# Projection groups of four parts over four PSUM banks in a one-core decoder step

## What is computed

```python
def run_trunk(x, mem_k, mem_v, states, P):
        y, mix_state = mixer_block(rmsnorm(x, P['norm_mix'][l]), ...)      # GLA, mLSTM, S5 branches
        x = x + y                                                          # y = merged @ w_out
        x = x + cross_attn(rmsnorm(x, P['norm_cross'][l]), mem_k[l], mem_v[l], P['w_cq'][l], P['w_co'][l])
        f, conv_state = conv_ffn(rmsnorm(x, P['norm_ffn'][l]), s_conv, P['w_ffn_up'][l],
                                 P['ffn_conv_w'][l], P['ffn_conv_b'][l], P['w_ffn_down'][l])
        x = x + f
    y = rmsnorm(x, P['norm_final'])

# in mixer_block:
    merged = (sigmoid(za) * (y_a @ w_branch_a) + sigmoid(zb) * (y_b @ w_branch_b)
              + sigmoid(zc) * (y_c @ w_branch_c))                          # the "branch gates"
```

## Time and profile before

| | us |
|---|---|
| median of 3 runs | 2227.8 |
| lowest and highest run | 2226.13, 2229.34 |
| span of the profiled execution | 2224.6 |
| TensorE matmul busy in it | 2183.2 (98%) |
| VectorE busy | 1157.5 (52%) |
| ScalarE busy | 605.2 (27%) |
| GpSimd busy | 281.4 (13%) |

### The profile page before, as it was taken

One profiled execution on the slowest core, in us unless ns is written; L12 is line 12 of the kernel. 1 busy time (PEld: TensorE's weight loads), 2 busy tenths in 40 slices (PEclk: granted clock), 3 DMA queues, 4 the chain that ended last, 5 costly groups with the idle time before them and its releaser, 6 DMA issues.

```text
span 2224.6 us, 34095 instructions
## 1 busy us (share of the span) xinstructions
PE 2183.2 (98%) x14582; PEld 2137.4 (96%) x14582; DVE 1157.5 (52%) x1336; ACT 605.2 (27%) x765; POOL 281.4 (13%) x436
## 2 busy tenths in 40 slices
PE   7999999999999999999999999999999999999997
PEld 6999999999999999999999988999999999999997
DVE  6514755344455354245643234456566665656657
ACT  6313344233322322333322144221111111111113
POOL 6689910000000000000000000000000000000001
PEclk9999999999999999999999999999999999999998
DMA  7322114212422223245312161111111111111112
GB/s 277 114 76 69 63 59 170 78 68 84 148 98 77 86 74 111 76 162 181 124 48 77 46 257 75 39 58 48 48 48 48 48 41 48 46 48 48 48 48 81
DMA packets 51872, 191.39 MB, mean 86 GB/s; under 512 B 5984, under 2 KB 11424, under 8 KB 48528
## 3 DMA queue, kind: packets, MB, share of 16 engines
q1 hardware_dynamic: 39232, 125.47, 16.5%
q0 software_dynamic: 10496, 46.66, 5.6%
q10 hardware_dynamic: 2016, 17.35, 2.0%
HBM read 152.53 MB, written 35.93 MB: 85 GB/s over the span
## 4 chain that ended last, share of the span: by engine, by line
PE 93%; DVE 4%; ACT 1%; DMA 1%; issue 1%; POOL 0%; DVEq 0%; ACTq 0%; POOLq 0%
PE ps L272 27%; PE ps L273 26%; PE ps L275 26%; PE ps L1939 1%; PE ps L2291 1%; PE ps L2267 1%; DVE WL L266 1%; DMA WRAW<-in_wslabs 1%; PE ps L2301 1%; ACT WH L261 1%; DVE XR L2781 0%; PE ps L1123 0%; PE ps L1124 0%; PE ps L1118 0%; DVE T L1009 0%
## 5 line engine op out<-in xcount | busy, mean ns | idle before, releaser
L272 PE MATMUL ps<-XH,WH 128*128 128x344 f32 x1752 | 563.5, 324 | 5.1 <-ACT STAGE L331 2.8
L273 PE MATMUL ps<-XL,WH 128*128 128x344 f32 x1560 | 495.1, 320 | 0.0
L272 PE MATMUL ps<-XN,WH 128*128 128x344 f32 x1224 | 391.0, 321 | 0.2 <-DVE WL L266 0.2
L273 PE MATMUL ps<-XN,WH 128*128 128x344 f32 x1224 | 389.3, 321 | 0.0
L275 PE MATMUL ps<-XH,WL 128*128 128x344 f32 x1752 | 371.4, 320 | 0.0
L266 DVE TENSOR_TENSOR WL<-WRAW,WH 128x1024 fp32r<-128x1024 f32 x177 | 220.8, 1248 | 277.0 <-ACT WH L261 276.3
L272 PEld LDWEIGHTS ps<-XH,WH 128*128 128x128 f32 x1752 | 330.2, 188 | 13.8 <-issue 9.3
L261 ACT ACTIVATE WH<-WRAW 128x1024 fp32r<-128x1024 f32 x177 | 186.6, 1054 | 517.6 <-PE ps L275 499.3
L273 PEld LDWEIGHTS ps<-XL,WH 128*128 128x128 f32 x1560 | 294.3, 189 | 0.1
L275 PEld LDWEIGHTS ps<-XH,WL 128*128 128x128 f32 x1752 | 293.6, 188 | 0.0
L275 PE MATMUL ps<-XN,WL 128*128 128x344 f32 x1224 | 259.0, 319 | 0.0
(11 more groups left out here) (542 smaller groups left out, 3163.8 us busy)
## 6 DMA issues: line engine op xcount, KB each, us to landing
WRAW<-in_wslabs SPq DMA_DIRECT2D x177, 512.0 KB, 3.5
scratch_spill<-STAGE SPq DMA_DIRECT2D x40, 516.0 KB, 2.7
ZS<-scratch_spill POOLq DMA_DIRECT2D x24, 516.0 KB, 5.4
XIN<-in_xT SPq DMA_DIRECT2D x8, 516.0 KB, 4.5
XR<-in_xT ACTq DMA_DIRECT2D x2, 2064.0 KB, 8.8
out_y<-XR SPq DMA_DIRECT2D x12, 344.0 KB, 2.5
CACHES<-in_ck ACTq DMA_DIRECT2D x4, 1024.0 KB, 14.2
CACHES<-in_cv ACTq DMA_DIRECT2D x4, 1024.0 KB, 16.0
```

The lines of the kernel that those rows point to most:

```text
L272: pe.matmul(out[t], WH[:, slot, w, :], xh(k, t), start=(k == 0), stop=False)
L273: pe.matmul(out[t], WH[:, slot, w, :], xl(k, t), start=False, stop=False)
```

## The change

From the branch gates on, most groups are made of `WIDE` = 4 parts of 258 columns in four banks, so slot 0 has banks 0 to 3 and slot 1 banks 4 to 7, all eight. A step of such a group has twelve matmuls and twelve weight loads. Helpers take the number of parts. Still of three parts are: all groups before the gates, the last group of `w_out` and of `w_co`, the first two and the last of the query projection, the first two of `w_co`, the first two of the FFN, and the last chunk's down product. Since slot 1 now holds banks 6 and 7, TensorE waits for `norm_rb` before the first four-part group of the query projection and of the FFN. VectorE's loop over the query groups is written out.

```diff
-TG, NTG = 344, 3
+TG, NTG, WIDE = 344, 3, 4
-        def acc(slot):
-            return ps[:, 3 * slot:3 * slot + 3, 0:TG]
-        def t3(ap):
-            return ap.rearrange("p (a b) -> p a b", b=TG)
+        def acc(slot, parts=NTG):
+            return ps[:, parts * slot:parts * (slot + 1), 0:N // parts]
+        def t3(ap, parts=NTG):
+            return ap.rearrange("p (a b) -> p a b", b=N // parts)
         def split_step(pe, out, slot, xh, xl, w, k, nk):
-            for t in range(len(out)):
-                pe.matmul(out[t], WH[:, slot, w, :], xh(k, t), start=(k == 0), stop=False)
-                pe.matmul(out[t], WH[:, slot, w, :], xl(k, t), start=False, stop=False)
-            for t in range(len(out)):
-                last = pe.matmul(out[t], WL[:, slot, w, :], xh(k, t), start=False, stop=(k == nk - 1))
+            parts = len(out)
+            for t in range(parts):
+                pe.matmul(out[t], WH[:, slot, w, :], xh(k, t, parts), start=(k == 0), stop=False)
+                pe.matmul(out[t], WH[:, slot, w, :], xl(k, t, parts), start=False, stop=False)
+            for t in range(parts):
+                last = pe.matmul(out[t], WL[:, slot, w, :], xh(k, t, parts), start=False, stop=(k == nk - 1))
+        def banks(slot, parts=NTG):
+            return [ps[:, parts * slot + t, 0:N // parts] for t in range(parts)]
+        def cols(t, parts=NTG):
+            return slice(t * (N // parts), (t + 1) * (N // parts))
...
         def pe_out(pe):
-            pe_start(pe, SL_OUT, G_OUT, 2, xl_cols)
-            pe_project(pe, SL_OUT + 2, G_OUT + 2, KT - 2)
+            pe_start(pe, SL_OUT, G_OUT, 2, xl_cols, WIDE)
+            pe_project(pe, SL_OUT + 2, G_OUT + 2, KT - 3, parts=WIDE)
+            pe_project(pe, SL_OUT + KT - 1, G_OUT + KT - 1, 1)
         def pe_cross(pe):
             pe_entry(pe, SL_CQ, G_CQ, 2, 3)
-            pe_project(pe, SL_CQ + 2, G_CQ + 2, KT - 3, next_hi_cols, next_lo_cols)
+            pe.wait_ge(norm_rb, 1)
+            pe_project(pe, SL_CQ + 2, G_CQ + 2, KT - 3, next_hi_cols, next_lo_cols, WIDE)
...
-            pe_project(pe, SL_CO + 2, G_CO + 2, KT - 2, xh_cols, xlo_cols)
+            pe_project(pe, SL_CO + 2, G_CO + 2, KT - 3, xh_cols, xlo_cols, WIDE)
+            pe_project(pe, SL_CO + KT - 1, G_CO + KT - 1, 1, xh_cols, xlo_cols)
...
-            with dve.Fori(0, KT // 2 - 1) as i:
+            for i in range(KT // 2 - 1):
                 for s in range(2):
                     query_group(i, s)
...
-                    split_product(pe, banks((g + k) % 2), (n + k) % 2, next_hi_cols, next_lo_cols, 0, KT).then_inc(acc_ready, 1)
+                    split_product(pe, banks((g + k) % 2, WIDE), (n + k) % 2, next_hi_cols, next_lo_cols, 0, KT).then_inc(acc_ready, 1)
...
             pe_entry(pe, SL_FFN, G_FFN, 3, 5)
+            pe.wait_ge(norm_rb, 2)
             up(0, SL_FFN, G_FFN, 0, 0, 2)
```

More of the change, by code:

```diff
@@ L282, in split_product, with xh_cols, xl_cols @@
             return last
-        def xh_cols(k, t):
-            return XH[:, k, t * TG:(t + 1) * TG]
-        def xl_cols(k, t):
-            return XL[:, k, t * TG:(t + 1) * TG]
-        def banks(slot):
-            return [ps[:, 3 * slot + t, 0:TG] for t in range(NTG)]
+        def xh_cols(k, t, parts=NTG):
+            return XH[:, k, cols(t, parts)]
+        def xl_cols(k, t, parts=NTG):
+            return XL[:, k, cols(t, parts)]
+        def banks(slot, parts=NTG):
+            return [ps[:, parts * slot + t, 0:N // parts] for t in range(parts)]
+        def cols(t, parts=NTG):
+            return slice(t * (N // parts), (t + 1) * (N // parts))
         fl_ready, fl_free, fl_stored = sem("fl_ready"), sem("fl_free"), sem("fl_stored")
@@ L397, in pe_start @@
                         pe.wait_ge(xl_ready, KT * ks + k + 1)
-                    last = split_step(pe, banks(g % 2), n % 2, xh_cols, xl, k, k, KT)
+                    last = split_step(pe, banks(g % 2, parts), n % 2, xh_cols, xl, k, k, KT)
                 last.then_inc(acc_ready, 1)
@@ L686, in keys @@
                         pe.wait_ge(xl_ready, k + 1)
-                    last = split_step(pe, [ps[:, g % 6, 0:MEM]], g % 2, lambda k, t: MEMH[:, k, :],
-                                      lambda k, t: MEML[:, k, :], k, k, KT)
+                    last = split_step(pe, [ps[:, g % 6, 0:MEM]], g % 2, lambda k, t, parts: MEMH[:, k, :],
+                                      lambda k, t, parts: MEML[:, k, :], k, k, KT)
                 last.then_inc(acc_ready, 1)
@@ L2067, in dve_gates @@
                         dve.wait_ge(z_sig, j + 1)
-                        nc.vector.tensor_tensor(t3(tmp if b else mg), t3(tmp), acc(slot), ALU.mult).then_inc(acc_free[slot], 1)
+                        nc.vector.tensor_tensor(t3(tmp if b else mg, WIDE), t3(tmp, WIDE), acc(slot, WIDE), ALU.mult).then_inc(acc_free[slot], 1)
                         dve.wait_ge(acc_free[slot], (g + s) // 2 + 1)
@@ L2132, in dve_next @@
                 x = XR[:, m, :]
-                nc.vector.tensor_tensor(t3(x), t3(x), acc(g % 2), ALU.add).then_inc(acc_free[g % 2], 1)
+                parts = WIDE if m in wide else NTG
+                nc.vector.tensor_tensor(t3(x, parts), t3(x, parts), acc(g % 2, parts), ALU.add).then_inc(acc_free[g % 2], 1)
                 dve.wait_ge(acc_free[g % 2], g // 2 + 1)
@@ L2186, in dve_out @@
             dve.wait_ge(x_again, 16)
-            dve_next(dve, st, SL_OUT, G_OUT, 2, 3, 2, x_again)
+            dve_next(dve, st, SL_OUT, G_OUT, 2, 3, 2, range(0, KT - 1), x_again)
         QXF = low("QXF", [128, KT * N], 8 * N)
@@ L2438, in query_group @@
                 g = G_CQ + s
+                parts = WIDE if i else NTG
                 dve.wait_ge(acc_ready, i * 2 + (g + 1))
-                nc.vector.scalar_tensor_tensor(out=t3(QXF[:, bass.ts(i * 2 + s, N)]), in0=acc(g % 2),
-                                               scalar=256.0 ** -0.5, in1=t3(RB[:, :]), op0=ALU.mult,
+                nc.vector.scalar_tensor_tensor(out=t3(QX[:, i * 2 + s, :], parts), in0=acc(g % 2, parts),
+                                               scalar=256.0 ** -0.5, in1=t3(RB[:, :], parts), op0=ALU.mult,
                                                op1=ALU.mult).then_inc(acc_free[g % 2], 1)
@@ L2493, in dve_cross @@
             dve_split(dve, 4, QX, XLO)
-            dve_next(dve, st, SL_CO, G_CO, 3, 5, 3)
+            dve_next(dve, st, SL_CO, G_CO, 3, 5, 3, range(2, KT - 1))
         HH = low("HH", [128, 2, 2, N], 2 * N, F32R)
@@ L2726, in up @@
                     dve.wait_ge(u_slots, i * per_t + (tile + k + 1))
-                    nc.vector.tensor_tensor(t3(UB[:, k % 2, 2:N + 2]), acc((g + k) % 2), t3(RB[:, :]),
+                    parts = NTG if whole and k < 2 else WIDE
+                    nc.vector.tensor_tensor(t3(UB[:, k % 2, 2:N + 2], parts), acc((g + k) % 2, parts), t3(RB[:, :], parts),
                                             M).then_inc(acc_free[(g + k) % 2], 1)
```

39 lines of the change are left out of this document (20 added, 19 removed).

## The result

| | before | after |
|---|---|---|
| median, us | 2228.17 (4 runs) | 2245.12 (4 runs) |
| lowest and highest, us | 2226.13, 2229.34 | 2240.12, 2245.90 |
| span of the profiled execution, us | 2224.6 | 2238.0 |

The changed kernel is slower: the ratio after to before is 1.0073, with an interval of 1.0059 to 1.0088. A second measurement of it is the last experiment. The prediction had 2193.3 us.

A forecast was written before the change was run, and what follows sets the result against it. TensorE, busy for 98% of the span, was taken as the bound. 728 steps, each 47.4 ns less (1372.8 against 1420.2), made 34.5 us less: span 2190.1, median 2193.3 us, range 2184 to 2262.

The forecast's parts named there:

- What a 258-column matmul costs: All changed steps: 114.4 ns a matmul, taken from the 256-column row as nearest; bounds 113.5 and 122.0 to 123.0.
- The two bursts of the earlier trace: 256-column matmuls at 20.97 to 23.13 and 25.39 to 27.43 us: 113.7 and 113.3 ns each, taken as 113.5.
- the break-even of 118.35: Changed steps: twelve matmuls must each cost under 1420.2 / 12 = 118.35 ns, or the change is a loss.
- the 106 ns of the earlier trace: One-column matmuls, 1.70 us for 16: a matmul bringing its own weights doesn't come under about 106 ns.
- B: Every changed step: each matmul loses a constant of about 15 ns; 43.8 ns more a step, 2259.7 us; chance 27%.
- pieces of 16 columns: B's other form: moving operand taken in 16-column pieces, 258 columns being 17 at 7.17 ns, so 121.9 ns a matmul.
- C: Changed steps: small fixed part, same at both lengths; 117.9 to 119.1 ns a matmul, 2223 to 2237 us; chance 10%.
- D: TensorE gains per matmul but stalls for slots or slabs and gives it back; 2201 to 2228 us; chance 5%.
- The count of 728 steps: Gates 96, `w_out` 56, queries 40, `w_co` 40, FFN up 336, FFN down 160: together 728 changed steps.
- the new wait for `norm_rb`: Before the first four-part query groups and in the FFN: over 2.9 us before it could hold, so cost nothing.
- a fourth row in PSUM: VectorE reads four rows of 258 for three of 344: nothing visible; even 50 ns more each would be hidden.
- The slots in `down`: FFN down, the tightest place: VectorE frees slots in time with some 0.6 us left; losing that cover would cost 7.6 us.

The follow-up runs named there:

- the bench: Kernel before plus 56 dense runs of 56 fp32r matmuls behind its last output, at widths 128 to 512: 117.2 ns each at 256 columns, 119.9 at 258.
- the kernel in place: Kernel after, each of the four parts computed 256 columns wide from its old start: 2234.13 us, ratio 1.0030 to the kernel before.
- the last kernel: Kernel before with parts of 260, 512 and 260 columns in one row of PSUM over three banks: 2221.38 us, ratio 0.9970.

## Why the prediction was wrong

**The step that failed** is "What a 258-column matmul costs". It took 114.4 ns, and 119.8 were measured. Everything hung on it, as the prediction said ("no other step of the sum can turn its sign"): 5.4 ns too low, times 12 matmuls, times 728 steps is 47.2 us, and that is nearly all of the 47.9 from 2190.1 to the span of 2238.0.

It failed in two ways, and the first could have been avoided. The two bursts of the earlier trace rows were both in the fast of the two speeds that 256 columns have, and I took their mean as the price of that length. The same code from 31.18 to 33.65 us has 117.6 ns; from there, with the same ns for two more columns, 258 come to 118.6, at the break-even of 118.35 and not 4 ns below it. The bench shows 117.2 for its typical run, and the kernel in place 118.7. The second failure is that from 113.5 I read the three lengths as "not on a line" and chose the point against the line. With 117.2 they lie near one: 5.7 ns + 0.4405 ns a column gives 118.5, 157.2 and 231.2, where the bench has 117.2, 157.2 and 231.2.

A third reading was wrong, though the sum did not use it: the 106 ns of the earlier trace rows as the floor of a matmul with its own weights. `pe_entry` issues 8 matmuls at L2155, and the trace has 16 records for them, so they are plain fp32, which leaves two for each, as in the bench. The first two records stand 28 ns apart and the others 111.6, and the 106 was the mean of both. For fp32r the bench has 110.7 ns at 128 columns and 112.7 at 240, so at 256 columns the cheaper of the two speeds, 113.3 to 113.6, is nearly on that flat stretch. To that extent the prediction's picture of 256 columns was right; that 258 would lie there too was not.

**The rivals.** B named the right direction and the right mechanism, a fixed part that twelve matmuls pay more often than nine, and the right doubt (the row of 256 columns as an exception). Its size was wrong: 15 ns was read as fixed, since the columns were taken at 0.417 ns; measured are 5.7 fixed and the rest proportional, so 17.4 ns a step and not 43.8. Its other form, pieces of 16 columns, fell in the bench. C's range, 117.9 to 119.1 ns and 2223 to 2237 us, ended 0.7 ns short, and its "within 5 us" was too narrow for its own upper price (119.1 ns gives 6.6 us); with its "small constant" it was the best description, and I had given it 10%. D didn't happen. The range of 2184 to 2262 holds the time only because it reached to B; that is no merit of the sum.

The rule of the Trainium skill, page "TensorE: Matmul & The Clock Gate", section "Back-to-back issue gap", N / 2.4 + 2.5 ns, would have had the sign right, with an estimate of 6 us. The section calls this the gap of an isolated matmul, and not that of a stream with weight loads. Its size does not agree with these runs of fp32r with a weight load each: it gives 145.8 ns at 344 columns and 215.8 at 512, where 157.2 and 231.2 were measured.

**What held.** The count of 728 steps: exact, by 2184 more matmuls. Nothing else in the sum cost or gained anything: the new wait for `norm_rb` was over before it could hold. ScalarE's copy, which gives the signal, ends at 1208.63 us (first line), `WL` at 1211.09, and the first four-part group starts at 1211.22:

```profile
1208.45 0.18 ACT L2181 ACTIVATE RB<-ps 128x8 f32<-128x8 f32 x1 [3.37 <-PE ps L2170]
...
1209.87 1.22 DVE L266 TENSOR_TENSOR WL<-WRAW,WH 128x1024 fp32r<-128x1024 f32 x1
...
1211.22 0.39 PE L273 MATMUL ps<-XN,WH 128*128 128x258 f32 x1
```

VectorE's adds of a group are 80 of 1228 ns against 80 of 1227, so a fourth row in PSUM costs nothing that shows. The slots in `down` came free in time: the one wait of TensorE on the `XR` add is 1.5 us, as in the earlier trace rows. With groups longer and not shorter, its slack was never tested in the direction that I had worked out.

**What stays open.** Why fp32r takes 0.44 ns a column at the full clock; what the two speeds at 256 columns are; the surplus over the steps' share, up to 2.6 us, in the runs that were not profiled; and whether the gain of the last kernel comes from its lengths or its starts. Of the first, it is shown that the width of the weight block, the data, the bank and the weight's address are not the cause.

## What to carry over

Where TensorE is full and the columns stay the same, an edit that changes the number of matmuls costs (fixed part) x (change in count). Here the fixed part is about 6 ns: 17.4 ns for three more matmuls in a step, and 5.7 ns by the bench. So splitting evenly into more parts loses, by 0.7% in this kernel. With the count held, parts of 260, 512 and 260 columns gained 0.3%. When a sum hangs on one duration, read it from every stretch that has it, not from two that agree; here a later burst of the same instructions stood 4 ns higher, which was all of the margin. A regression on a mean is no stand-in for reading where the time went: the mean clock also counts time in which nothing waits for the engine. And before a price is taken that breaks a line through the others, see whether it is the price that is odd.

## What the runs showed of the hardware that was not expected

- A dense stream of fp32r matmuls, each with its weight load, at a granted clock of 1.00: 5.7 ns + 0.4405 ns a column from 256 to 512 columns, within 1.5 ns, and 110.7, 112.2 and 112.7 ns at 128, 192 and 240.
- At 256 columns such a stream runs at 113.3 to 113.6 or at 117.6 to 117.9 ns a matmul, over some 20 to 70 matmuls at a time. In one kernel, with all else equal, a matmul of 290 or 350 columns just before led to the fast one, one of 264, 320 or 400 to the slow one. It was not seen at 344.
- Where the moving operand starts matters by up to 3 ns: 256 columns cost 117.2 and 116.7 ns from columns 0 and 256, 118.3 from 4 and 516, 120.0 from 2, 258 and 774.
- The width of the weight block (128, 64 or 32 columns) changes a 258-column matmul by less than 1 ns (119.9, 119.7, 119.1), and zeros in the moving operand change nothing (156.0 ns at 344 columns either way).
- Plain fp32 matmuls leave two records each in the trace: 112 for 56, 289.2 ns apart at 344 columns.
- One VectorE instruction reads 1032 columns across two PSUM bank borders in 1.23 us, as it does from three or four separate rows.
- The granted clock has dips ahead of the gates (down to 0.74, taken over 20 us), in varying places. Most of the spread of a kernel's runs goes with the mean clock: 1.94 us for 0.001 of it, with 0.8 us left over.
